# Two-layer transformer stack on one core: projections and gate tiles as three reduced-precision products, one fill tile and the bias table moved

## The reference, cut to what matters

```
proj = h @ w_in                      # 3072 columns: dq dk dv (differential heads), sq sk sv
diff = softmax(dq dk) pairs, attn = p0 - lam * p1, times dv, RMS-normed
sb   = stick-breaking attention of sq, sk, sv
h = layer_norm(ALPHA * h + [diff, sb] @ w_o)
q = h @ w_query; two top-16 lists of 128 keys per head -> 16 of 16384 experts per head, gate = softmax
y = sum over chosen experts of gate * gelu(h . u_e) * v_e
h = layer_norm(ALPHA * h + y)
```

```
p = h @ w_in                         # 15 pieces: heads of three attentions, gate logits, low-rank inputs
o_nsa (with a relative-position bias table), o_mla, o_fox = three attentions
gates = sigmoid(h @ w_gate)          # 3072 columns
merged = g0 * (o_nsa @ w_a) + g1 * (o_mla @ w_b) + g2 * (o_fox @ w_c)
h = layer_norm(ALPHA * h + merged @ w_out)
h = layer_norm(ALPHA * h + cross_attention(h, mem))
h = layer_norm(ALPHA * h + relu(h @ w_up) ** 2 @ w_down)
```

## Time and profile before

| | |
|---|---|
| median of the runs | 3300.31 us |
| the profiled execution | 3307.39 us, its span 3305.5 us |
| PE busy | 3155.6 us (95% of the span) |
| PE weight loads busy | 2660.7 us (80%), beside the matmuls |
| DVE busy | 1785.8 us (54%) |
| ACT busy | 1181.0 us (36%) |
| mean granted TensorE clock | 0.966 of full speed |
| transfers | 490.39 MB read, mean 149 GB/s |

### The profile page before, as it was taken

How to read it: one execution, slowest core, us unless ns; L and a number is a source line. 1 busy time by engine, 2 the same in 40 slices (tenths; PEclk the granted TensorE clock), 3 DMA queues, 4 the chain that set the end, 5 groups by cost and what they waited for, 6 DMA issues and landing times.

```text
span 3305.5 us, 52615 instructions
## 1 busy us (share of the span) xinstructions
PE 3155.6 (95%) x19498; PEld 2660.7 (80%) x19498; DVE 1785.8 (54%) x3599; ACT 1181.0 (36%) x1876; POOL 1.8 (0%) x6
## 2 busy tenths in 40 slices
PE   8899899999999989999999999899998999999898
PEld 6678689898897758878989899687766978776697
DVE  1368964787657137796478755613334461333446
ACT  1321344444444132134444444312224441222444
POOL 0000000000000000000000000000000000000000
PEclk9999999999999999999999999898998999899899
DMA  4244155543554314325554455452233454223344
GB/s 187 77 153 153 65 191 181 192 156 147 190 189 179 140 65 165 140 81 192 185 191 144 163 190 189 157 188 78 77 140 128 182 180 180 83 77 134 132 180 153
DMA packets 68022, 493.51 MB, mean 149 GB/s; under 512 B 7576, under 2 KB 7584, under 8 KB 8352
## 3 DMA queue, kind: packets, MB, share of 16 engines
q1 hardware_dynamic: 67568, 490.42, 40.8%
q0 software_dynamic: 304, 1.06, 0.1%
HBM read 490.39 MB, written 1.06 MB: 149 GB/s over the span
## 4 chain that ended last, share of the span: by engine, by line
PE 89%; DVE 5%; issue 3%; ACT 2%; DVEq 1%; DMA 1%; SPq 0%; POOL 0%; ACTq 0%; POOLq 0%
PE ps L231 12%; PE ps L641 9%; PE ps L642 9%; PE ps L643 8%; PE ps L241 8%; PE ps L611 7%; PE ps L612 7%; PE ps L613 7%; PE ps L248 3%; PE ps L267 2%; PE ps L293 2%; PE ps L1524 2%; DVE hots L1223 2%; PE ps L921 2%; PE ps L1367 1%
## 5 line engine op out<-in xcount | busy, mean ns | idle before, releaser
L727 DVE TENSOR_TENSOR ring_l<-ring,tile_h 128x1024 fp32r<-128x1024 f32 x572 | 675.0, 1222 | 591.3 <-ACT tile_h L683 591.3
L683 ACT ACTIVATE tile_h<-ring 128x1024 fp32r<-128x1024 f32 x572 | 573.5, 1052 | 453.4 <-PE ps L643 453.4
L611 PE MATMUL ps<-x_h,tile_h 128*128 128x256 f32 x2016 | 575.5, 285 | 0.8 <-DVE ring_l L727 0.8
L612 PE MATMUL ps<-x_l,tile_h 128*128 128x256 f32 x2016 | 570.0, 283 | 0.0
L613 PE MATMUL ps<-x_h,ring_l 128*128 128x256 f32 x2016 | 569.9, 283 | 0.0
L231 PE MATMUL ps<-xT,ring 128*128 128x256 f32 x1792 | 390.1, 379 | 0.0
L611 PEld LDWEIGHTS ps<-x_h,tile_h 128*128 128x128 f32 x2016 | 386.4, 192 | 1.8 <-issue 1.6
L612 PEld LDWEIGHTS ps<-x_l,tile_h 128*128 128x128 f32 x2016 | 386.5, 192 | 0.2
L613 PEld LDWEIGHTS ps<-x_h,ring_l 128*128 128x128 f32 x2016 | 386.3, 192 | 0.0
L231 PEld LDWEIGHTS ps<-xT,ring 128*128 128x128 f32 x1792 | 339.4, 190 | 45.6
L641 PE MATMUL ps<-tile_h,w_even 128*128 128x512 f32 x640 | 251.7, 393 | 15.0 <-DVE w_even L749 15.0
(11 more groups left out here) (283 smaller groups left out, 3802.5 us busy)
## 6 DMA issues: line engine op xcount, KB each, us to landing
ring<-stream SPq DMA_DIRECT2D x464, 1024.0 KB, 4.8
cs<-consts SPq DMA_DIRECT2D x1, 1712.5 KB, 8.5
x<-x_in SPq DMA_DIRECT2D x1, 1024.0 KB, 4.9
arena<-scratch POOLq DMA_DIRECT2D x1, 1024.0 KB, 6.0
out<-x SPq DMA_DIRECT2D x2, 512.0 KB, 2.7
tab<-table SPq DMA_DIRECT2D x1, 1.0 KB, 8.3
scratch<-arena POOLq DMA_DIRECT2D x1, 12.0 KB, 1.8
```

The lines of the kernel that those rows point to most:

```text
L611: nc.tensor.matmul(out, uh[:, c, f], x_h[:, c, :], start=(c == 0), stop=False)
L612: nc.tensor.matmul(out, uh[:, c, f], x_l[:, c, :], start=False, stop=False)
L683: nc.scalar.activation(tile_h[:, j % 2, n], slot(k + j)[:, n], ACT.Copy).then_inc(hi_ready, 1)
L727: nc.vector.tensor_tensor(low_of(k + j)[:, n], slot(k + j)[:, n], tile_h[:, j % 2, n].bitcast(F32), ALU.subtract).then_inc(lo_ready, 1)
```

## The change: what it does, and the diff

- Block 1: projection tiles 1 to 5 of each layer are computed in three passes (`pe_project`), with ACT's and DVE's split ahead of them; tile 0 stays plain. Of the six tiles that filled the units, five stay there (10 matmuls a unit), and the sixth (`A_PROJ + 11`, plain) is computed after the stick-breaking scores, into bank 0.
- Block 2: projection tiles 1 to 10 in three passes; tile 0 and the 64-column tile 11 stay plain. The twelve gate tiles in three passes inside the units; their weights are split by halves, one half a unit (`gate_high` on ACT behind the copy of the transposes, `gate_low` on DVE behind the normalizing), and PE goes chunk by chunk through both feature halves.
- `x_h` and `x_l` are now made twice a layer, at its start and before the experts or the MLP.
- The bias table: the small product, the copy and the transfer to device memory stand at the start of the program (DVE waits there for `t_out`); POOL reads the bands back once the last block of expert products in three passes that reads `x_h` is done, into the space of `x_h`. The flips stay where they were.
- Arrays of block 2 are laid out anew so that none lies where `tile_h`, `x_h` or `x_l` is in use.

```
+        def pe_project(pe, kind, k, s, j, bank):
+            pe.wait_ge(lo_ready, 2 * s + (2 * j + 2))
+            wh, wl = tile_chunks(tile_h[:, j % 2, :]), tile_chunks(low_of(k + j))
+            for a in range(2):
+                part = slice(a * P, (a + 1) * P)
+                out = ps[bank][:, a * SEQ:(a + 1) * SEQ]
+                for c in range(KC):
+                    if kind == "features":
+                        three = ((wh[:, c, part], x_h[:, c, :]), (wh[:, c, part], x_l[:, c, :]),
+                                 (wl[:, c, part], x_h[:, c, :]))
+                    else:
+                        three = ((x_h[:, c, part], wh[:, c, :]), (x_h[:, c, part], wl[:, c, :]),
+                                 (x_l[:, c, part], wh[:, c, :]))
+                    for m, (lhs, rhs) in enumerate(three):
+                        ins = nc.tensor.matmul(out, lhs, rhs, start=(c == 0 and m == 0), stop=(c == KC - 1 and m == 2))
...
+        def act_high_half(act, k, j, hf):
+            n = slice(1024 * hf, 1024 * hf + 1024)
+            nc.scalar.activation(tile_h[:, j % 2, n], slot(k + j)[:, n], ACT.Copy).then_inc(hi_ready, 1)
+        def dve_low_half(dve, k, s, j, hf):
+            n = slice(1024 * hf, 1024 * hf + 1024)
+            dve.wait_ge(hi_ready, 2 * s + (2 * j + hf + 1))
+            nc.vector.tensor_tensor(low_of(k + j)[:, n], slot(k + j)[:, n], tile_h[:, j % 2, n].bitcast(F32),
+                                    ALU.subtract).then_inc(lo_ready, 1)
...
# pe_block1
+            pe.wait_ge(xl_ready, 2 * l + 1)
             for j in range(1, 6):
-                arrived(pe, 1, l, k)
                 if j >= 4:
                     pe.wait_ge(proj_ev, l * 12 + (j - 3))
-                (up_features if j < 4 else up_tokens)(chunks(k), xT, 4 + j % 4).then_inc(tile_done, 1)
+                pe_project(pe, "features" if j < 4 else "tokens", A_PROJ, l * SPLIT_A - 1, j,
+                           4 + j % 4).then_inc(tile_done, 1)
...
-                at = 12 * u + 6 * part
-                for n, m in (divmod(a, 16) for a in range(at, at + 6)):
+                at = 10 * u + 5 * part
+                for n, m in (divmod(a, 16) for a in range(at, at + 5)):
...
             for h in range(8):
                 sb_scores(h)
+            arrived(pe, 1, l, A_PROJ + 11)
+            pe.wait_ge(o_copied, l * TT + 1)
+            up_tokens(chunks(A_PROJ + 11), xT, 0).then_inc(tile_done, 1)
...
             pe.wait_ge(mix_ready, l * TT + TT)
+            pe.wait_ge(proj_ev, l * 12 + 12)
...
# act_block1 (block 2 alike, with act.wait_ge(t_flip, 1) ahead of the split)
+            act.wait_ge(xt_ready, 4 * KC * l + 2 * KC)
+            act_split_x(act)
+            act_high(act, 1, l, A_PROJ, 0, 1)
             act.wait_ge(lam_sum, l + 1)
...
             for j in range(6):
+                if j + 2 < 6:
+                    act_high(act, 1, l, A_PROJ, 0, j + 2)
                 proj_out(j, 4 + j % 4)
...
                 nc.scalar.activation(e, e, ACT.Ln, bias=1.0).then_inc(z_log, 1)
+            proj_out(11, 0)
...
# dve_block1
+            dve_split_x(dve, 2 * l)
+            for j in range(1, 6):
+                dve_low(dve, A_PROJ, l * SPLIT_A - 1, 0, j)
             dve.wait_ge(lam_exp, l + 1)
...
# gate_run (block 2, PE), for each n, m and with c, fb = divmod(m, 2)
+                    if m % 8 == 0:
+                        pe.wait_ge(lo_ready, 2 * gs + (2 * n + m // 8 + 1))
...
+                    nc.tensor.matmul(out, wh[:, c, part], x_h[:, c, :], start=(m == 0), stop=False,
+                                     skip_group_check=True)
+                    nc.tensor.matmul(out, wh[:, c, part], x_l[:, c, :], start=False, stop=False, skip_group_check=True)
+                    last = nc.tensor.matmul(out, wl[:, c, part], x_h[:, c, :], start=False, stop=(c == KC - 1),
...
# act_block2: gate_high(0), gate_high(1) behind the copies of kc_ev; then
+            def high_after(u):
+                if u == 0:
+                    gate_high(4)
+                if u <= 18:
+                    gate_high(u + 5)
+            gate_high(2)
+            gate_high(3)
+            act_units(act, done_b + l * UNITS_B, mix_units, between_units, high_after)
...
# dve_block2, at the start of a layer
+            dve_split_x(dve, 2 * LAYERS + 2 * l)
+            for j in range(1, 3):
+                dve_low(dve, B_PROJ, LAYERS * SPLIT_A + l * SPLIT_B - 1, 0, j)
             step.after(nc.vector.memset(xb.rearrange("p l s g n -> p (l s g n)"), 0.0))
+            for j in range(3, 5):
+                dve_low(dve, B_PROJ, LAYERS * SPLIT_A + l * SPLIT_B - 1, 0, j)
             dve.wait_ge(b_ev, l * 12 + 3)
...
+            for j in range(5, 11):
+                dve_low(dve, B_PROJ, LAYERS * SPLIT_A + l * SPLIT_B - 1, 0, j)
...
# dve_block2, units
+            def low_after(u):
+                if u <= 1:
+                    gate_low(2 * u + 2)
+                    gate_low(2 * u + 3)
+                elif u <= 19:
+                    gate_low(u + 4)
+            gate_low(0)
+            gate_low(1)
+            dve_units(dve, step, done_b + l * UNITS_B, mix_units, plain_scale, low_after)
...
# POOL
             pool.wait_ge(t_out, 16)
+            pool.wait_ge(tile_done, (LAYERS - 1) * A_TILES + (A_EXP + 7 * BLK + 1))
+            pool.dma_start(band_in.rearrange("p (h k) -> p h k", h=8), band).then_inc(t_in, 16)
...
# PE, start of the program (ACT's copy to bd moves with it; DVE waits for t_out)
             pe.wait_ge(loaded, 48)
+            nc.tensor.matmul(ps[0][0:8, 0:384], tab[:, :], cs[0:32, CONST["bucket"]], start=True,
+                             stop=True).then_inc(t_mm, 1)
             pe_turn_x(pe)
```

More of the change, by code:

```diff
@@ L78 @@
 EARLY = 12
-SPLIT_A = 2 * PAIRS - BLK
-SPLIT_B = 2 * MLP_PAIRS - 1
+PROJ_A, PROJ_B = 5, 10
+SPLIT_A = PROJ_A + 2 * PAIRS - BLK
+GATE_B = 12
+SPLIT_B = PROJ_B + GATE_B + 2 * MLP_PAIRS - 1
 CONST = {}
@@ L440, in pe_units, with act_units @@
                     fill(u, 1)
-        def act_units(act, base, units, fill_out=None):
+        def act_units(act, base, units, fill_out=None, after=None):
             def exps(u):
@@ L465, in act_units, with dve_units @@
                                      ACT.Copy).then_inc(pt_ev, 1)
-        def dve_units(dve, step, base, units, scale_probs):
+                if after is not None:
+                    after(u)
+        def dve_units(dve, step, base, units, scale_probs, after=None):
             def bias(u):
@@ L896, in pe_block1 @@
             g = l * PAIRS
-            s = l * SPLIT_A
+            s = l * SPLIT_A + PROJ_A
             def plain_up(i, j):
@@ L967, in act_block1 @@
             for j in range(6):
+                if j + 2 < 6:
+                    act_high(act, 1, l, A_PROJ, 0, j + 2)
                 proj_out(j, 4 + j % 4)
             def proj_done(u):
-                for n in range(6):
-                    if (16 * n + 15) // 12 == u - 1:
+                for n in range(5):
+                    if (16 * n + 15) // 10 == u - 1:
                         proj_out(6 + n, (7, 2, 3)[n % 3])
@@ L1492, in pe_block2 @@
             pe.wait_ge(ct_ev, l * 4 + 4)
+            gs = LAYERS * SPLIT_A + l * SPLIT_B + PROJ_B
             def gate_run(at, count):
-                n, m = at // 16, at % 16
-                if m == 0:
-                    arrived(pe, 2, l, B_GATE + n)
-                    if n:
+                for n, m in (divmod(a, 16) for a in range(at, at + count)):
+                    c, fb = divmod(m, 2)
+                    if m == 0 and n:
                         pe.wait_ge(fill_ev, l * 12 + n)
-                last = up_piece("features", chunks(B_GATE + n), xT, 7, m, m + count)
-                if m + count == 16:
-                    last.then_inc(tile_done, 1)
+                    if m % 8 == 0:
+                        pe.wait_ge(lo_ready, 2 * gs + (2 * n + m // 8 + 1))
+                    wh, wl = tile_chunks(tile_h[:, n % 2, :]), tile_chunks(low_of(B_GATE + n))
+                    part, out = slice(fb * P, (fb + 1) * P), ps[7][:, fb * SEQ:(fb + 1) * SEQ]
+                    nc.tensor.matmul(out, wh[:, c, part], x_h[:, c, :], start=(m == 0), stop=False,
+                                     skip_group_check=True)
+                    nc.tensor.matmul(out, wh[:, c, part], x_l[:, c, :], start=False, stop=False, skip_group_check=True)
+                    last = nc.tensor.matmul(out, wl[:, c, part], x_h[:, c, :], start=False, stop=(c == KC - 1),
+                                            skip_group_check=True)
+                    if m == 15:
+                        last.then_inc(tile_done, 1)
             def gate_piece(u, part):
@@ L1823, in _ @@
             act.sem_inc(gate_ev, 2)
+            act.wait_ge(t_mm, 1)
+            nc.scalar.activation(bd[0:8, :], ps[0][0:8, 0:384], ACT.Copy).then_inc(t_ev, 1)
             for tt in range(TT):
@@ L1827, in _ @@
                 act_block1(act, l)
-            act.wait_ge(t_mm, 1)
```

(1 more changed line is left out.)

84 lines of the change are left out of this document (49 added, 35 removed).

## The result

The changed kernel takes 3216.99 us, the median of 4 runs (3216.33 to 3224.23). The kernel before, run once more beside it (3310.39 us), now has a median of 3305.35 us over four runs. The ratio is 0.9736, 95% interval 0.9716 to 0.9756: 88 us less; it leaves out the run of 6194.93 us, which took almost twice as long as the others. The forecast was 3220 us, between 3203 and 3250, faster. The profiled execution took 3216.33 us, span 3214.5 us, 91.0 us less than the span before.

The account below looks back on a forecast made before the run. PE was taken to bound the kernel. Projections 33.9 + gates 25.4 + fill 13.8 + table 7.5 - 1.0 at the start = 79.6 us saved, giving 3220 us against the median 3300.31; range 3203 to 3250.

Parts of the forecast that it names:

- What bounds the kernel: Whole kernel: PE, busy 95% of the span; only less time in its products or fewer gaps between them can pay.
- Projections, 33.9 us: Layer starts of both blocks: 30 tiles in three passes, each 5.78 us instead of 6.91, save 33.9 us.
- The term for the starts: First split tiles: 1.0 us lost at program start (bounds 0 and 3), nothing in layer 1 of both blocks.
- Gates, 25.4 us: Block 2's units: 24 gate tiles in three passes save 27.1 us, less 1.7 for the last units; net 25.4.
- Fill, 13.8 us: Gap after stick-breaking scores: the moved 6.91 us tile fits, saving 13.8 us in all, bounds 3.8 and 17.6.
- Table, 7.5 us net: Between the blocks: 10.96 us removed, less 2.6 of PE waiting and 0.8 for the clock; bounds 5.7 and 11.
- the wait of PE moves on: Start of block 2: with the table's round trip gone, PE stands 2.6 us for the split after tile 0.
- (a): Block 2's units: a chain of latencies, not PE's, so the gates give nothing; 3245 us, chance 0.11.
- (b): Projections: PE starves on late splits or transfers, so their 34 us are gone; 3254 us, chance 0.08.
- (c): ACT and DVE queues in the units: halves and softmax form one chain, slower; 3434 us, chance 0.04.
- (d): Moved parts take no effect: fill extends its gap, table's 9.5 us return as PE's wait; 3235 us, chance 0.09.
- (e): Unrolled stretches: three passes cost three quarters of plain, 5.18 us a tile; 3188 us, chance 0.04.

Follow-up runs that it names:

- u_gates: Changed kernel with block 2's twelve gate tiles a layer in plain f32 again, without the splitting of their halves; 3248.37 us.
- x_two: Changed kernel with one of a gate tile's three passes left out (rounded weights with the low part of x); single run, 3179.53 us.
- u_table: Changed kernel with the bias table's product, copy and round trip through memory between block 1 and block 2 again; 3231.62 us.
- u_proj: Changed kernel with all projection tiles at the start of a layer in plain f32 again, x still split there; 3241.25 us.
- x_dve1: Changed kernel with one more unused VectorE subtraction (1.22 us) in each of 24 mixed units a layer; first unit to first branch tile 140.43 us.
- n_fills: Changed kernel with block 1's five unit fill tiles also in three passes, four ACT copies and two DVE halves ahead of the first bias; 3214.73 us.

## Why the prediction was right, step by step

- **What bounds the kernel.** Right: every cut of PE's own work came out in the time at its full length, in the units too (the runs `u_gates` and `x_two`).
- **Projections, 33.9 us.** Measured 27.9 against before and 30.3 by the undo. The term for the starts was too small: in layer 0 of block 1 the first three-pass tile starts at 23.75 us behind a wait of 1.57 us, where the second plain tile started at 21.93, and the first three-pass tile of block 2 took 7.33 us in place of 5.76, partly at half clock, behind the wait of 2.67 us. Of this the forecast had 2.6 + 0.8 us, but under the table, and 1.0 us for the program's start; the early table is not the cause, since without it (`u_table`) the tile starts at 23.80. In layer 1 of both blocks, for which it took nothing, there is indeed no wait. That the steady state costs nothing held: no wait between later tiles.
- **Gates, 25.4 us.** Measured 27.7. The mis-sized term is the 1.7 us written off for the last units: their transposes wait 0.25 and 0.42 us where one waited 0.19, and the shorter products were saved nevertheless. No cost of code fetch shows, as taken.
- **Fill, 13.8 us.** Measured 14.2 by the undo, 15.2 against before; the 1.0 us between them lies in the units ahead of the gap, where half clock fell on other instructions. Behind the gap the clock gave back 0.5 and 0.1 us against before, taken as 0 with an upper bound of 1.9 a layer: in layer 0 the sums still began at half clock, for 3.0 us where it was 4.2.
- **Table, 7.5 us net, and 1.0 us lost at the start.** This sum was too small by half: 13.6 us by the undo's trace. The wait of 2.6 us was foreseen in the right place and size (2.67), but "the wait of PE moves on" was wrong: it comes from the three-pass start of block 2 and stays with the table back (2.12). The second omission is the flips, which took 6.07 us in the earlier trace rows at half clock and take 3.44 now. The half clock began just ahead of the round trip, at 2126.6 in the kernel before and at 2104.6 in the undo, and lasted 17.1 us in both. The early table lost nothing at the start.
- **The clock.** The forecast had no term for stretches that the change does not touch. They gave some 6 us here and make single experiments differ from the sum of their stages by up to 8 us either way.
- **The whole.** The four undos cost 31.4 + 24.3 + 16.3 + 14.6 = 86.6 us, the change gained 88.4; the parts hardly interact, as far as these few us of clock let one see. The projections gave 6 us less and the table 6 us more than their terms, but more than half of both is one amount under another name: the wait and the slow tile at the start of block 2, which the forecast took off the table and the measurement counts under the projections. Like for like the projections gave 2.6 us less (27.9 for 33.9 - 3.4) and the table 3.2 us more (14.12 for 10.96). With gates, fill and start, each forecast 1 to 2.3 us too low, the terms come to 85 us where 79.6 were forecast, and the untouched stretches add 6. That the forecast of 3220 us lies 3 us from 3217 is in part luck: the gain was 9 us larger (88.4 for 79.6), and the base moved up by 5 (3305.35 for 3300.31).
- **Rivals.** (a) and (b) are out by `u_gates` and `u_proj`; (c) by `x_dve1`; (d) by the gap of 1.68 us in stick-breaking and by `u_table`, though its wait for the split is there at 2.67 us; (e), three quarters: a tile takes 5.76 us, 0.83 of the plain 6.91, and the pass left out costs 0.12 us a product. The count of passes of the Trainium skill (FP8 and Floating Point Precision, "TensorE Precision Notes"), from which the prediction took 0.75, does not give the time here; the trace disagrees with that ratio.

## What to carry to other kernels

When a trace shows that one engine holds a stage, price an edit by that engine's rate in a stage that already runs the new form, and check the other engines' slack by the time between their last result and its use; here the price of a tile was good to 0.02 us and the slack to about half a us a unit. Before work is put into a pipeline's units, ask what then stands ahead of the first unit: in `n_fills` that cost 1.2 and 2.2 of some 5.3 us a layer. After an edit read the granted clock of the stages behind it too, and compare by stages before by totals.

## What was not expected of the hardware

A wait of 0.70 us ahead of a stage of narrow products (60 columns) stood before a fall of TensorE's clock from 2.4 to 1.2 GHz that lasted 17.1 or 20.5 us and cost 7.9 us a layer in the changed kernel; 1.78 us of unused products in its place kept 2.4 GHz in all four layers seen. The Trainium skill (TensorE: Matmul & The Clock Gate, "Why this matters for your kernels") warns of long idle gaps between bursts of products; here the gap ahead of the fall was short, in 23 of 24 layers. What made the one layer stay up, whether the wait alone or the narrow products on both sides of it bring the fall, and whether wider products behind it would do as well, was not tried and stays open.
